# One kernel, one core: the last norm moved beside the last expert, and the down weights cut by FF tiles

## The chip, the cores and the metric

The kernel runs on one core of a Trainium2 chip. The metric is the device time of one execution in microseconds (us). TensorE (PE) multiplies, ScalarE (ACT) and VectorE (DVE) work on tiles, GpSimd (POOL) issues the indexed DMAs and now and then works on a tile, SyncE (SP) issues the other DMAs. Each engine runs its own instructions in program order and waits on semaphores.

## The reference

A two-layer backbone over 1024 latent and 256 context tokens of width D = 1024. What matters here is the second layer's mixture of experts and the last norm:

```python
aff = softmax(h @ router_w)                  # 1024 tokens, 16 experts
g, idx = top_k(swapaxes(aff, 1, 2), 128)     # each expert takes 128 tokens
xe = h[idx]
a, u = xe @ w_gate[e], xe @ w_up[e]          # 1024 -> 1408
y = (silu(a) * u) @ w_down[e]                # 1408 -> 1024
out = zeros.at[idx].add(y * g)
xl = xl + m_l[5] * out
return rmsnorm(xl, final_g)                  # per token: x / sqrt(mean(x*x) + eps) * final_g
```

A token can be taken by several experts or by none. Everything is float32; each product is made of three float32r products (high by high, high by low, low by high parts).

## The kernel before

The kernel is a row of stages with a barrier between them. The last three are choose_stage (top-k of the second layer, with FirstPieces beside it), expert_rows_stage (16 experts, called a turn each) and final_stage (the last norm).

In expert_rows_stage an expert's weights come as 12 pieces of 128x2816 words: a gate and an up piece for each of 4 units of 352 hidden columns, and four down pieces, each all 11 FF tiles by a quarter of the 1024 output columns. SP loads a piece into one of 5 raw places as soon as DVE has split the piece that lay there (L2235). ACT rounds it to its high part (L2360) and DVE subtracts to get the low part (L2421), into one of 4 places that PE frees four pieces later. PE takes the pieces in the order written in turn (L2332): gate 0, up 0, the four down pieces of the expert before, then gate and up of units 1 to 3. An up piece is 8 x 3 matmuls of 352 columns (L2288), a down piece 11 x 3 of 256 columns (L2304).

Between them stand transposes: turn_h (L2308) turns a unit's hidden rows h, and is followed by copy_h on ACT and split_h on DVE; it waits for multiply on DVE (L2433). turn_x (L2321) turns the gathered rows of the next expert, in the middle of the down pieces; copy_x and high_x on ACT and split_x on DVE (L2427) make its parts, double-buffered. POOL gathers the rows of expert e+1 (L2246) and scatters the weighted result of expert e-1 with an accumulating DMA into x_res in HBM (L2251); weigh on DVE (L2452) makes that result.

After the last scatter and a barrier, final_stage loads x_res in 8 tiles of 128 tokens into two places, squares and sums on ACT (L2854), takes the root on ACT (L2856), scales and multiplies on DVE (L2871, L2873) and stores.

Of the kernel before, what the change touches and what calls it, by code (L numbers as in the profile page):

```python
# [2092 lines left out]
ROW_UNITS, ROW_SLOTS, ROW_RAW = 4, 4, 5  # L2093
ROW_READY = ROW_SLOTS + ROW_RAW
ROW_U = FF // ROW_UNITS
ROW_PIECE = K * ROW_U
assert ROW_PIECE == FJ * (D // 4)


class RowBuffers:  # L2100
# [3 lines left out]
    def __init__(self, nc, ctx, m):  # L2104
# [3 lines left out]
        self.xg, self.xm = sb("xg", [P, D]), sb("xm", [P, D])  # L2108
        self.ys, self.gates = sb("ys", [P, D]), sb("gates", [P, D])
        self.x_hi, self.x_lo = (sb(x, [P, 2, K, P], F32R) for x in ("xhi", "xlo"))  # L2110
        self.h = sb("h", [P, FF])
        self.hT_hi, self.hT_lo = (sb(x, [P, FJ, P], F32R) for x in ("hthi", "htlo"))
        self.sa = m.rope[:, 0, 0:2 * ROW_U].rearrange("p (b n) -> p b n", b=2)
        self.gcur = sb("gcur", [P, 2])


class FirstPieces:
# [7 lines left out]

    def on_sync(self, sp):
        for n in range(ROW_READY):
# [4 lines left out]
            sp.dma_start(self.m.rows.raw[:, s, :], self.d["moe_rows"][n if n < 8 else 12]).then_inc(self.landed[s], 16)  # L2132
        for s in range(ROW_RAW):
            sp.wait_ge(self.landed[s], 16 * len(range(s, ROW_READY, ROW_RAW)))

    def on_scalar(self, act):
        r = self.m.rows
        for s in range(ROW_SLOTS):
            act.wait_ge(self.landed[s], 16)
            act.copy(r.high[:, s, :], r.raw[:, s, :]).then_inc(self.high_done, 1)  # L2140

    def on_gpsimd(self, pool):
        r = self.m.rows
        for s in range(ROW_SLOTS):
            pool.wait_ge(self.high_done, s + 1)
            pool.tensor_tensor(r.low[:, s, :], r.raw[:, s, :], r.high[:, s, :].bitcast(F32), ALU.subtract).then_inc(
                self.low_done, 1)
# [14 lines left out]
def expert_rows_stage(nc, m, d, name, layer):  # L2162
    UNITS, U, PIECE, SLOTS = ROW_UNITS, ROW_U, ROW_PIECE, ROW_SLOTS
    TURN = 12
    DOWN = range(2, 6)
    GROUPS = [range(0, 2), range(2, 5), range(5, 8), range(8, 11)]
    pieces = d["moe_rows"]
# [3 lines left out]
    with stage_of(nc) as ctx:  # L2171
        piece_done, high_done, low_done, sa_done, h_done, h_turned, hT_high, hT_low = semaphores(
            nc, ctx, " ".join(f"{name}_{x}" for x in "piece high low sa h hturn hthi htlo".split()))
        x_turned, x_read, x_high, x_low, y_read, ys_ready, gate_ready = semaphores(
            nc, ctx, " ".join(f"{name}_{x}" for x in "xturn xread xhi xlo yread ys gcur".split()))
        gates_in, gathered, scattered, x_parts = semaphores(
            nc, ctx, " ".join(f"{name}_{x}" for x in "gates gat scat xparts".split()))
# [3 lines left out]
        def prepared(e, p):  # L2181

            return isinstance(e, int) and e == 0 and p in (0, 1, 6, 7)

        def exists(e, p):

            return not isinstance(e, int) or (0 <= e < NE and not (e == 0 and p in DOWN)) or (e == NE and p in DOWN)

        def number(e, p):

            if isinstance(e, int) and e == 0 and p < DOWN[0]:
                return p + 1
            return e * TURN + (p + 1 - len(DOWN)) - (DOWN[0] if isinstance(e, int) and e == NE else 0)

        def before(e, p, places):

            while True:
                e, p = (e, p - places) if p >= places else (e - 1, p - places + TURN)
                if isinstance(e, int) and e < 0:
# [4 lines left out]
        def raw(e, p):  # L2204

            return r.raw[:, (number(e, p) - 1) % ROW_RAW, :]

        def landing(e, p):

            return piece_in[(number(e, p) - 1) % ROW_RAW], 16 * ((number(e, p) - 1) // ROW_RAW + 1)  # L2210

        def need(engine, sem, value):

            if value is not None and (not isinstance(value, int) or value > 0):
                engine.wait_ge(sem, value)

        def turns(engine, body):

            for e in range(NE + 1):
                body(e, e % 2)  # L2220

        def later(e):
# [788 lines left out]
```

## Time and profile before

| what | us |
|---|---|
| median of 3 runs | 3142.82 (3140.67 to 3143.96) |
| the profiled execution | 3143.25 |
| its span, first to last instruction | 3141.4 |
| PE busy in the span | 2829.9 (90%) |
| DVE, ACT, POOL busy | 2077.3, 1767.9, 630.1 |

The span is the stretch that the trace shows; the time of that execution is 1.85 us longer. A busy share is an average over stages with different limits, so each stage is read by itself.

### The profile page before, as it was taken

How to read it: one execution, taken by the hardware profiler on the slowest of the kernel's cores; microseconds unless marked ns; L12 is line 12 of the kernel's file. 1: busy time of each engine (PE TensorE's matmuls, PEld its weight loads, DVE VectorE, ACT ScalarE, POOL GpSimd, SP SyncE). 2: the span in 40 equal slices, each digit the busy share in tenths (PEclk: the TensorE clock that was granted, in tenths of full speed). 3: DMA queues.
4: the chain of work that ended last, by engine and by line, in shares of the span. 5: the costliest groups of instructions: out<-in, count | busy, mean ns of one | idle time of the engine just before them, and what ended most of it. 6: DMA issues, size and time to landing. Idle time of an engine off the chain costs nothing. (4 is left out here: it accounts for less than half of the span.)

```text
span 3141.4 us, 54667 instructions
## 1 busy us (share of the span) xinstructions
PE 2829.9 (90%) x23207; PEld 2423.5 (77%) x23207; DVE 2077.3 (66%) x2141; ACT 1767.9 (56%) x1876; POOL 630.1 (20%) x282
## 2 busy tenths in 40 slices
PE   6999897966999999999999689989469999999992
PEld 4788654755888888888888577757369999999992
DVE  3412555455677777777777358764668888888884
ACT  3111345443565656555655358874457777777764
POOL 3111232211111111111111056542301011011110
PEclk8999999987999999999999799999789999999996
DMA  5011362446887788778877410104569999999993
GB/s 218 28 40 32 145 229 77 148 165 234 302 309 285 284 310 309 286 282 309 311 286 276 169 34 31 41 13 166 195 229 366 388 377 369 391 369 381 380 364 121
DMA packets 139221, 726.41 MB, mean 231 GB/s; under 512 B 12226, under 2 KB 14946, under 8 KB 111202
## 3 DMA queue, kind: packets, MB, share of 16 engines
q1 hardware_dynamic: 126276, 684.99, 57.0%
q0 software_dynamic: 12288, 37.75, 4.8%
q8 instruction: 185, 3.03, 0.4%
q14 instruction: 56, 0.46, 0.0%
q10 hardware_dynamic: 416, 0.18, 0.0%
HBM read 680.90 MB, written 41.98 MB: 230 GB/s over the span
## 5 line engine op out<-in xcount | busy, mean ns | idle before, releaser
L1990 DVE TENSOR_TENSOR mixed_low<-mixed_raw,mixed_high 128x4096 fp32r<-128x4096 f32 (+1 forms) x142 | 576.4, 4059 | 216.9 <-ACT mixed_high L1920 216.8
L2421 DVE TENSOR_TENSOR rows_low<-rows_raw,rows_high 128x2816 fp32r<-128x2816 f32 x188 | 580.9, 3090 | 92.5 <-ACT rows_high L2360 88.6
L1920 ACT CAST mixed_high<-mixed_raw 128x4096 fp32r<-128x4096 f32 (+1 forms) x142 | 473.9, 3337 | 124.2 <-DMA mixed_raw<-in_moe 74.8
L2360 ACT CAST rows_high<-rows_raw 128x2816 fp32r<-128x2816 f32 x188 | 481.1, 2563 | 88.1 <-PE ps L2275 88.1
L2273 PE MATMUL ps<-rows_high,rows_xhi 128*128 128x352 f32 x1024 | 336.5, 329 | 4.5 <-issue 4.5
L2275 PE MATMUL ps<-rows_high,rows_xlo 128*128 128x352 f32 x1024 | 329.6, 322 | 0.0
L2274 PE MATMUL ps<-rows_low,rows_xhi 128*128 128x352 f32 x1024 | 328.8, 321 | 0.0
L1821 PE MATMUL ps<-mixed_high,mixed_xhi 128*128 128x512 f32 (+1 forms) x768 | 296.1, 386 | 3.5 <-DVE mixed_xlo L2006 3.5
L1822 PE MATMUL ps<-mixed_low,mixed_xhi 128*128 128x512 f32 (+1 forms) x768 | 286.6, 373 | 0.0
L1823 PE MATMUL ps<-mixed_high,mixed_xlo 128*128 128x512 f32 (+1 forms) x768 | 286.5, 373 | 0.0
L2273 PE MATMUL ps<-rows_high,rows_hthi 128*128 128x256 f32 x704 | 201.4, 286 | 3.0 <-issue 3.0
L2251 POOL DMA_INDIRECT x_res<-rows_ys,idx x16 | 68.0, 4249 | 677.8 <-DVEq L2455 677.8
L2274 PE MATMUL ps<-rows_low,rows_hthi 128*128 128x256 f32 x704 | 200.1, 284 | 0.0
L2275 PE MATMUL ps<-rows_high,rows_htlo 128*128 128x256 f32 x704 | 200.1, 284 | 0.0
L2273 PEld LDWEIGHTS ps<-rows_high,rows_xhi 128*128 128x128 f32 x1024 | 192.9, 188 | 4.9 <-issue 4.9
L2274 PEld LDWEIGHTS ps<-rows_low,rows_xhi 128*128 128x128 f32 x1024 | 193.6, 189 | 0.0
L2275 PEld LDWEIGHTS ps<-rows_high,rows_xlo 128*128 128x128 f32 x1024 | 192.5, 188 | 0.0
L1821 PEld LDWEIGHTS ps<-mixed_high,mixed_xhi 128*128 128x128 f32 x768 | 144.9, 189 | 41.8 <-issue 23.4
L1773 POOL DMA_INDIRECT x_res<-mixed_ys,idx x16 | 25.6, 1602 | 725.9 <-DVEq L2062 725.9
L1809 PE MATMUL ps<-mixed_raw,mixed_xc 128*32 128x128 f32 (+1 forms) x6144 | 164.0, 264 | 0.0
L1809 PEld LDWEIGHTS ps<-mixed_raw,mixed_xc 128*32 128x32 f32 x6144 | 152.0, 110 | 15.3 <-issue 15.3
L1823 PEld LDWEIGHTS ps<-mixed_high,mixed_xlo 128*128 128x128 f32 x768 | 144.8, 189 | 20.9
(351 smaller groups left out, 6282.5 us busy)
## 6 DMA issues: line engine op xcount, KB each, us to landing
rows_raw<-in_moe_rows SPq DMA_DIRECT2D x192, 1408.0 KB, 8.7
mixed_raw<-in_moe SPq DMA_DIRECT2D x96, 2048.0 KB, 12.5
mixed_raw<-in_moe SPq DMA_DIRECT2D x48, 1536.0 KB, 11.5
ring_r<-in_ada_w SPq DMA_DIRECT2D x19, 2048.0 KB, 8.0
mixed_raw<-in_ada_w SPq DMA_DIRECT2D x5, 2048.0 KB, 9.9
w_raw_r<-in_ev_in SPq DMA_DIRECT2D x18, 512.0 KB, 3.5
w_raw_u<-in_od_in SPq DMA_DIRECT2D x16, 512.0 KB, 3.7
x_res<-x_o SPq DMA_DIRECT2D x10, 512.0 KB, 2.6
```

Of the source, the lines that this page charges most:

```text
L1809: mm = pe.matmul(out, r.xc[:, owner % 2, k, :], w[:, :, k * P + 32 * g:k * P + 32 * g + 32], start=(k == 0), stop=(k == K - 1), tile_posit ...
L1821: pe.matmul(out, x_high_part, w_high_part, start=first, stop=False)
L1822: pe.matmul(out, x_high_part, w_low_part, start=False, stop=False)
L1823: return pe.matmul(out, x_low_part, w_high_part, start=False, stop=last)
L1920: act.copy(r.high[:, p % SLOTS, 0:nj, :], raw(e, p)).then_inc(high_done, 1)
L1990: dve.tensor_tensor(r.low[:, p % SLOTS, 0:nj, :], raw(e, p), r.high[:, p % SLOTS, 0:nj, :].bitcast(F32), ALU.subtract).then_inc(low_done, 1)
L2251: pool.indirect_dma_start(d["x_res"], bass.IndirectOffsetOnAxis(ap=m.idx[:, e:e + 1], axis=0), ys[:, :], None, compute_op=ALU.add).then_in ...
L2273: pe.matmul(out, x_high_part, w_high_part, start=first, stop=False)
L2274: pe.matmul(out, x_high_part, w_low_part, start=False, stop=False)
L2275: return pe.matmul(out, x_low_part, w_high_part, start=False, stop=last)
L2360: act.copy(high[:, p % SLOTS, :], raw(e, p)).then_inc(high_done, 1)
L2421: dve.tensor_tensor(low[:, p % SLOTS, :], raw(e, p), high[:, p % SLOTS, :].bitcast(F32), ALU.subtract).then_inc(low_done, 1)
```

## The change

The down weights of an expert are now cut by FF tiles into pieces of 2, 3, 3 and 3 tiles by all 1024 columns (the HBM layout stays, so a piece is loaded as 4 blocks of 2 or 3 KB per partition), and a matmul of a down piece is 512 columns wide. The order of pieces in a turn is gate 0, up 0, down 3 of the expert before, gate 1, up 1, down 0, gate 2, up 2, down 1, gate 3, up 3, down 2. turn_h follows each third piece; the two halves of turn_x follow the third and the sixth. The low part of x is single-buffered and made by POOL (low_x), but for expert 0, where DVE does it.

final_stage is gone. Beside the last expert, SP loads final_g and, after the scatter of the last expert but one, the 8 tiles of x_res into raw places that are free by then; ACT and DVE square them, DVE and POOL scale them, SP stores them. The last expert's result isn't scattered into x_res: POOL gathers its 128 rows of x_res, DVE adds and norms them (last_rows), and POOL writes them over the stored rows of out. FirstPieces loads 8 pieces (9 before) and splits 3 (4 before).

The diff, cut to its core:

```diff
+ROW_UNITS, ROW_SLOTS, ROW_RAW, ROW_SPLIT, ROW_TURN = 4, 4, 5, 3, 12
+ROW_READY = ROW_SPLIT + ROW_RAW
...
+ROW_J = [range(0, 2), range(2, 5), range(5, 8), range(8, 11)]
+ROW_PIECE = 3 * D
+QUARTER = D // 4
+ROW_GATE, ROW_UP, ROW_DOWN = (0, 3, 6, 9), (1, 4, 7, 10), (5, 8, 11, 2)
...
+def load_row_piece(sp, d, r, e, p):
+    kind, u = ROW_GROUP[p]
+    to = r.raw[:, (row_number(e, p) - 1) % ROW_RAW, 0:row_columns(p)]
+    if kind < 2:
+        return sp.dma_start(to, d["moe_rows"][e * 12 + 2 * u + kind])
+    at = (e - (p == 2)) * 12 + 8
+    j = ROW_J[u]
+    src = d["moe_rows"][at:at + 4, :, j[0] * QUARTER:(j[-1] + 1) * QUARTER].rearrange("q p n -> p q n")
+    return sp.dma_start(to.rearrange("p (q n) -> p q n", q=4), src)
...
+        self.x_hi, self.x_lo = sb("xhi", [P, 2, K, P], F32R), sb("xlo", [P, K, P], F32R)
+        self.hT_hi, self.hT_lo = (sb(x, [P, 2, 3, P], F32R) for x in ("hthi", "htlo"))
+        self.xm = m.rope[:, 1, :]
...
+        def last_place(i):
+            n = number(NE, 2) - 4 + i // 3
+            return n, r.raw[:, (n - 1) % ROW_RAW, (i % 3) * D:(i % 3 + 1) * D]
+        gain = last_place(0)[1]
+        tiles = [last_place(1 + t)[1] for t in range(LT)]
+        junk = xm
+        stat = m.mask[:, 0:4 * 16].rearrange("p (x t) -> p x t", x=4)
+        ON_DVE_SQUARE, ON_POOL = (2, 5), (1, 4, 7)
...
+            sp.wait_ge(low_done, splits(last_place(0)[0]))
+            sp.dma_start(gain, d["final_g"].to_broadcast((P, D))).then_inc(gain_in, 16)
+            sp.wait_ge(scattered, 16 * (NE - 1))
+            for t in range(LT):
+                sp.wait_ge(low_done, splits(last_place(1 + t)[0]))
+                sp.dma_start(tiles[t], d["x_res"][t * P:(t + 1) * P, :]).then_inc(x_in[t], 16)
+            for t in range(LT):
+                pooled = sum(x in ON_POOL for x in range(t + 1))
+                if t in ON_POOL:
+                    sp.wait_ge(out_pool, pooled)
+                else:
+                    sp.wait_ge(out_dve, t + 1 - pooled)
+                sp.dma_start(d["out"][t * P:(t + 1) * P, :], tiles[t]).then_inc(stored, 16)
+            sp.wait_ge(stored, 16 * LT)
...
+            def low_x(e):
+                pool.wait_ge(x_high, e + 1)
+                pool.wait_ge(piece_done, number(e - 1, ROW_UP[-1]))
+                flat = lambda x: x.rearrange("p k n -> p (k n)")
+                pool.tensor_tensor(flat(x_lo[:, :, :]), xm, flat(x_hi[:, e % 2, :, :]).bitcast(F32),
+                                   ALU.subtract).then_inc(x_low, 1)
...
+                if followed(e):
                     gather(e + 1)
                 if e:
                     scatter(e - 1)
-            scatter(NE - 1)
-            pool.wait_ge(scattered, 16 * NE)
+                if followed(e):
+                    low_x(e + 1)
+            pool.wait_ge(scattered, 16 * (NE - 1))
+            pool.wait_ge(x_turned, 2 * NE)
+            pool.indirect_dma_start(xg[:, :], None, d["x_res"], bass.IndirectOffsetOnAxis(
+                ap=m.idx[:, NE - 1:NE], axis=0)).then_inc(picked, 16)
+            pool.wait_ge(gain_in, 16)
+            pool.wait_ge(inverse_done, 1)
+            for t in ON_POOL:
+                pool.tensor_scalar(tiles[t], tiles[t], stat[:, 3, t:t + 1], None, ALU.mult).then_inc(chain, 1)
+                pool.wait_ge(chain, ON_POOL.index(t) + 1)
+                pool.tensor_tensor(tiles[t], tiles[t], gain, ALU.mult).then_inc(out_pool, 1)
+            pool.wait_ge(stored, 16 * LT)
+            pool.wait_ge(rows_added, 1)
+            pool.indirect_dma_start(d["out"], bass.IndirectOffsetOnAxis(ap=m.idx[:, NE - 1:NE], axis=0),
+                                    ys[:, :], None).then_inc(rows_out, 16)
+            pool.wait_ge(rows_out, 16)
             pool.wait_ge(gathered, 16 * NE)
...
+                    wh, wl = (w.rearrange("p (q j n) -> p j q n", q=4, n=QUARTER) for w in (wh, wl))
+                    steps = [(i, half) for i in range(len(ROW_J[u])) for half in range(2)]
+                    if e == NE:
+                        steps.sort(key=lambda step: step[1])
+                    for i, half in steps:
+                        j = ROW_J[u][i]
+                        at = slice(2 * half, 2 * half + 2)
+                        out = m.ps[:, 4 + half, :].rearrange("p (q n) -> p q n", q=2)
+                        mm = products(out, hT_hi[:, t % 2, i, :], hT_lo[:, t % 2, i, :],
+                                      wh[:, i, at, :], wl[:, i, at, :], j == 0, j == FJ - 1)
+                        if e == NE and (i, half) == (len(ROW_J[u]) - 1, 0):
+                            mm.then_inc(piece_done, 1)
...
+            for half in range(2):
+                turn_x(0, half)
+            for e in range(NE + 1):
+                for p in range(TURN):
+                    if exists(e, p):
+                        latent(e, p)
+                    if p % 3 == 2 and expert(e):
+                        turn_h(e, p // 3)
+                    if p in (2, 5) and followed(e):
+                        turn_x(e + 1, p // 3)
...
+                    t = UNITS * e + p // 3
+                    if p % 3 == 0 and 0 < t:
+                        copy_h(t - 1)
+                    if p % 3 == 0:
+                        silu(e, p // 3)
+                    if p in (4, 7) and followed(e):
+                        copy_x(e + 1, p // 7)
+                    if p == 8 and followed(e):
+                        high_x(e + 1)
+                    if followed(e) or p < 8:
+                        split(*following(e, p))
+                    if not followed(e) and p == 7:
+                        square(0)
+                        square(1)
+                    if not followed(e) and p == 8:
+                        split(NE, 2)
+                        square(3)
+            for t in (4, 6, 7):
+                square(t)
+            root(1, slice(0, LT))
+            copy_h(UNITS * NE - 1)
+            root(2, slice(LT, LT + 1))
...
+            def give(t):
+                dve.scalar_tensor_tensor(tiles[t], tiles[t], stat[:, 3, t:t + 1], gain, ALU.mult, ALU.mult).then_inc(out_dve, 1)
+            def last_rows():
+                part_sum = lambda i: stat[:, i, LT + 1:LT + 2]
+                dve.wait_ge(gate_ready, NE)
+                dve.wait_ge(picked, 16)
+                for half in range(2):
+                    at = slice(half * BANK, (half + 1) * BANK)
+                    dve.wait_ge(piece_done, number(NE, 2) + half)
+                    dve.scalar_tensor_tensor(ys[:, at], m.ps[:, 4 + half, :], gcur[:, 0:1], gates[:, at],
+                                             ALU.mult, ALU.mult).then_inc(y_read, 1)
+                    dve.wait_ge(y_read, e * 2 + half + 1)
+                    dve.tensor_tensor(xg[:, at], xg[:, at], ys[:, at], ALU.add).then_inc(y_read_b, 1)
+                    dve.wait_ge(y_read_b, 2 * half + 1)
+                    dve.tensor_tensor_reduce(ys[:, at], xg[:, at], xg[:, at], 1.0, 0.0, ALU.mult, ALU.add,
+                                             part_sum(half)).then_inc(sq_dve, 1)
+                    dve.wait_ge(sq_dve, len(ON_DVE_SQUARE) + half + 1)
+                    if half == 0:
+                        dve.tensor_scalar(part_sum(2), part_sum(0), 1.0 / D, EPS, ALU.mult, ALU.add).then_inc(y_read_b, 1)
+                        dve.wait_ge(y_read_b, 2)
+                dve.scalar_tensor_tensor(stat[:, 1, LT:LT + 1], part_sum(1), 1.0 / D, part_sum(2), ALU.mult, ALU.add).then_inc(
+                    mean_done, 1)
+                inverse(2, slice(LT, LT + 1))
+                dve.scalar_tensor_tensor(ys[:, :], xg[:, :], stat[:, 3, LT:LT + 1], gain, ALU.mult, ALU.mult).then_inc(
+                    rows_added, 1)
...
+            first_x()
+            dve.wait_ge(gates_in, 16)
+            for p in range(SLOTS):
+                split(0, p)
+            for e in range(NE):
                 for p in range(TURN):
+                    t = UNITS * e + p // 3
+                    if p % 3 == 0 and 0 < t:
+                        split_h(t - 1)
+                    if not followed(e) and p == 10:
+                        square(5)
+                    if p % 3 == 1:
+                        multiply(e, p // 3)
+                    if p == 2 and 0 < e:
+                        weigh(e - 1)
+                    if followed(e) or p < 8:
+                        split(*following(e, p))
+                    if not followed(e) and p == 8:
+                        dve.wait_ge(scattered, 16 * (NE - 1))
+                        square(2)
+                        split(NE, 2)
+            dve.wait_ge(y_read, 2 * (NE - 1))
+            dve.tensor_copy(gcur[:, 0:1], m.gate[:, NE - 1:NE]).then_inc(gate_ready, 1)
+            dve.wait_ge(sq_act, LT - len(ON_DVE_SQUARE))
+            dve.wait_ge(sq_dve, len(ON_DVE_SQUARE))
+            dve.tensor_scalar(stat[:, 1, 0:LT], stat[:, 0, 0:LT], 1.0 / D, EPS, ALU.mult, ALU.add).then_inc(mean_done, 1)
+            dve.wait_ge(gain_in, 16)
+            inverse(1, slice(0, LT))
+            give(0)
+            split_h(UNITS * NE - 1)
+            for t in range(1, LT):
+                if t not in ON_POOL:
+                    give(t)
+            last_rows()
...
-            (m.plain, lambda: final_stage(nc, m, d)),
```

## Rows read from the trace of the kernel before

**Rows 1.** The page: span, and busy time, share and instructions of PE.

```profile
span 3141.4 us, 54667 instructions
...
PE 2829.9 (90%) x23207; PEld 2423.5 (77%) x23207; DVE 2077.3 (66%) x2141; ACT 1767.9 (56%) x1876; POOL 630.1 (20%) x282
```

**Rows 2.** Busy time by stretch, one turn: PE, PEld, DVE, ACT, POOL, clock, DMA share, GB/s.

```profile
2390.83:2439.53 48.70, 48.70 (x346) 48.39 (x344) 42.80 (x25) 37.20 (x30) 6.94 (x2) 1.00 0.98 372
```

**Rows 3.** Timeline of POOL in the experts: start, us, what, idle before.

```profile
2464.08 4.42 POOL L2251 DMA_INDIRECT x_res<-rows_ys,idx  x1 [41.44 <-DVEq L2455]
2468.80 2.53 POOL L2246 DMA_INDIRECT rows_xg<-x_norm,idx  x1 [0.30 <-issue]
...
2999.76 4.43 POOL L2251 DMA_INDIRECT x_res<-rows_ys,idx  x1 [41.49 <-DVEq L2455]
```

**Rows 4.** Timeline of PE: 256 columns here, 512 in the first layer.

```profile
3030.33 0.28 PE L2273 MATMUL ps<-rows_high,rows_hthi 128*128 128x256 f32 x1
...
3040.05 0.28 PE L2273 MATMUL ps<-rows_high,rows_hthi 128*128 128x256 f32 x1
...
1252.59 0.39 PE L1821 MATMUL ps<-mixed_high,mixed_hthi 128*128 128x512 f32 x1
...
1255.54 0.39 PE L1822 MATMUL ps<-mixed_low,mixed_hthi 128*128 128x512 f32 x1
```

**Rows 5.** Groups of instructions, experts: busy us, mean ns, idle before, releasers.

```profile
L2421 DVE TENSOR_TENSOR rows_low<-rows_raw,rows_high 128x2816 fp32r<-128x2816 f32 x188 | 580.9, 3090 | 92.5 <-ACT rows_high L2360 88.6 <-DVE rows_ys L2452 3.2
L2360 ACT CAST rows_high<-rows_raw 128x2816 fp32r<-128x2816 f32 x188 | 481.1, 2563 | 88.1 <-PE ps L2275 88.1
L2433 DVE TENSOR_TENSOR rows_h<-ps,rope_sb 128x352 f32<-128x352 f32 x64 | 33.2, 518 | 11.3 <-PE ps L2275 9.5 <-issue 1.8
```

**Rows 6.** Timelines of DVE and POOL where the two meet.

```profile
2467.39 3.09 DVE L2421 TENSOR_TENSOR rows_low<-rows_raw,rows_high 128x2816 fp32r<-128x2816 f32 x1
...
2096.23 1.49 DVE L2763 SCALAR_TENSOR_TENSOR B_second<-B_second 128x1280 f32<-128x1280 f32 x1 [11.69 <-POOL B_second L2714]
2097.64 3.03 DVE L2784 TENSOR_TENSOR C_second<-C_second,B_second 128x1024 f32<-128x1024 f32 x1
...
2096.32 3.26 POOL L2709 TENSOR_TENSOR B_second<-B_second 128x1024 f32<-128x1024 f32 x1
```

**Rows 7.** Groups of POOL's instructions on tiles, other stages.

```profile
L537 POOL TENSOR_TENSOR w_lo_u<-w_raw_u,w_hi_u 128x1024 fp32r<-128x1024 f32 x12 | 28.8, 2399 | 20.4 <-ACT w_hi_u L532 20.4
...
L1093 POOL TENSOR_SCALAR A_r<-A_r,C_first 128x640 f32<-128x640 f32 x16 | 29.9, 1886 | 59.9 <-DVE C_first L1131 59.9
```

**Rows 8.** The gathers of either layer: duration min/median/max in ns; issue to landing.

```profile
L2246 POOL DMA_INDIRECT rows_xg<-x_norm,idx x16: 947/2510/2536, 2289.6 to 2955.8; - x16
...
DMA to landing us min/median/max: 4.3/15.9/17.2
...
L1766 POOL DMA_INDIRECT mixed_xg<-x_norm,idx x16: 947/1009/1723, 738.8 to 1615.7; - x16
...
DMA to landing us min/median/max: 4.2/5.8/7.5
```

**Rows 9.** DMA from 2400 to 2900 us: rate in 40 slices, one queue, weight loads.

```profile
GB/s 378 306 389 424 411 277 405 421 383 307 420 420 356 317 423 407 357 325 425 413 345 333 429 406 339 347 424 407 327 355 425 406 316 373 424 395 304 378 422 403
...
q1 hardware_dynamic: 17778, 178.02, 89.5%
...
rows_raw<-in_moe_rows SPq DMA_DIRECT2D x123, 1408.0 KB, 8.7
```

**Rows 10.** Timelines of PE, SP and DVE, the end; groups of the last norm.

```profile
3067.27 0.32 PE L2275 MATMUL ps<-rows_high,rows_xlo 128*128 128x352 f32 x1
...
3103.88 0.81 SPq L2829 DMA_DIRECT2D A_s<-x_res  x2
...
3136.65 1.23 DVE L2873 TENSOR_TENSOR A_s<-A_s 128x1024 f32<-128x1024 f32 x1
...
L2854 ACT ACTIVATE A_s<-A_s 128x1024 f32<-128x1024 f32 x8 | 8.4, 1055 | 7.3 <-DMA A_s<-x_res 7.3
```

More of the change, by code:

```diff
@@ L2162, in expert_rows_stage @@
 def expert_rows_stage(nc, m, d, name, layer):
[L2163 to L2167, printed above, removed]
+    UNITS, U, SLOTS, TURN = ROW_UNITS, ROW_U, ROW_SLOTS, ROW_TURN
+    exists, number = row_exists, row_number
     r = m.rows
@@ L2349, in _ @@
-            turn_x(0)
-            turns(pe, turn)
+                if kind == 0:
+                    need(pe, h_done, t - 1)
+                elif kind == 2:
+                    pe.wait_ge(hT_high, t + 1)
+                    pe.wait_ge(hT_low, t + 1)
+                    if u == 0:
+                        need(pe, y_read, e * 2)
+                need(pe, high_done, splits(number(e, p)))
+                need(pe, low_done, splits(number(e, p)))
+                wh, wl = (w[:, part(e, p), 0:row_columns(p)] for w in (high, low))
@@ L2354, in split @@
             def split(e, p):
-                if not exists(e, p) or prepared(e, p):
-                    return
-                act.wait_ge(*landing(e, p))
-                need(act, piece_done, before(e, p, SLOTS))
-                act.copy(high[:, p % SLOTS, :], raw(e, p)).then_inc(high_done, 1)
+                if exists(e, p) and number(e, p) > ROW_SPLIT:
+                    sem, value = landing(e, p)
+                    need(act, sem, value)
+                    need(act, piece_done, part_freed(e, p))
+                    act.copy(high[:, part(e, p), 0:row_columns(p)], raw(e, p)).then_inc(high_done, 1)
             def copy_x(e, half):
@@ new lines, in square, with root @@
+            def square(t):
+                act.wait_ge(x_in[t], 16)
+                done = sum(x not in ON_DVE_SQUARE for x in range(t))
+                if done:
+                    act.wait_ge(sq_act, done)
+                else:
+                    act.wait_ge(x_low, NE)
+                act.activation(junk, tiles[t], ACT.Square, accum_out=stat[:, 0, t:t + 1]).then_inc(sq_act, 1)
+            def root(n, at):
+                act.wait_ge(mean_done, n)
+                act.activation(stat[:, 2, at], stat[:, 1, at], ACT.Sqrt).then_inc(root_done, 1)
@@ L2429, in multiply @@
-            def multiply(e, p, u):
-                dve.wait_ge(sa_done, e * UNITS + (u + 1))
-                dve.wait_ge(piece_done, number(e, p))
-                need(dve, h_turned, (e - 1) * UNITS + (min(u + 1, 3) + 1))
+                if exists(e, p) and number(e, p) > ROW_SPLIT:
+                    dve.wait_ge(high_done, splits(number(e, p)))
+                    need(dve, piece_done, part_freed(e, p))
+                    dve.tensor_tensor(low[:, part(e, p), 0:row_columns(p)], raw(e, p),
+                                      high[:, part(e, p), 0:row_columns(p)].bitcast(F32), ALU.subtract).then_inc(low_done, 1)
```

390 lines of the change are left out of this document (144 added, 246 removed).

## The prediction

> **What bounds the kernel now.** I read four views: the page, then the busy times of one turn, then the waits of that turn, then its ends. The page gives PE 90% of the span [rows 1], which is a mean over stages and decides nothing. The scatters of the experts lie (2999.76 − 2464.08) / 11 = 48.70 us apart [rows 3], and in a window of that length PE is busy for all of it, at the full clock, while DVE has 42.80 and ACT 37.20 [rows 2]. So PE sets the turn, and DVE has about 6 us of slack. The groups agree: ACT's casts wait for PE to free a place and never for a DMA; DVE's splits wait for ACT, hardly for a landing [rows 5]. The DMA engines are busy 98% [rows 2], which looks like a bound, but a turn's 372 GB/s x 48.7 us = 18.1 MB would take 42.7 us at the 424 GB/s of the best slice [rows 9]: they are full because the queue runs ahead. The other thing to see is the end: the last up piece ends at 3067.27 + .16 = 3067.4 and the span at 3141.4, 74.0 us later, filled by four down pieces, a scatter, a barrier and the last norm, whose first load is issued only at 3103.88 [rows 10]. So a gain can come from PE's work in a turn and from these 74 us; the losses can come from whatever makes PE wait.
>
> **PE's work.** A matmul of 256 columns takes (3040.05 − 3030.33) / 81 = .120 us, one of 512 columns (2.95 / 13) = .227 [rows 4]. An expert's down pieces are now 4 x 33 = 132 of the first, 15.84 us, and become 11 x 2 x 3 = 66 of the second, 14.98: .86 less. Up to the last up piece PE did 15 experts' down pieces, 237.6 us; now it does these and 5 of 11 FF tiles of the last expert, 15.45 x 14.98 = 231.5. That is **−6.1**. Up pieces and the number of transposes stay.
>
> **Edit A, low_x on POOL.** The low part of x is now single-buffered, so it can be made only when up 3 of the expert before has ended, and gate 0 of the next expert waits for it. Between them lie one down piece of 3 tiles (18 x .227 = 4.1) and a turn_h, about 4.4 us. A POOL subtract of this shape and type took 2.40 [rows 7], which would fit. But POOL and DVE hold each other up when both read two tiles: a POOL multiply whose start a DVE step of 1.49 had preceded lasted 3.26, about 1.9 beyond that step's end, and the DVE multiply beside it lasted 3.03 instead of the 1.23 of the same size at the end [rows 6, 10]. DVE's splits are such steps, 3.09 long [rows 5], and run nearly back to back. In my hand schedule of the new turn up 3 ends at 43.5 us, the split then running goes from 42.6 to 45.7, low_x takes 45.7 to 48.0 and gate 0 could start at 47.6. I take .5 us for each of the 15 followed turns: **+7.5**. Lower bound: no wait, 0. Upper: low_x lasts 3.09 + 2.40 + its share of a second split, some 6.4 against 4.4, 2 us a turn, +30. I stay near the lower, because a POOL step that came second got in right behind the running one [rows 6]. The split behind low_x slips to 51.3, and DVE has the slack for it.
>
> **Edit B, the gather.** In the new POOL order a turn's scatter is followed by low_x, and then by the next gather, so the gather starts up to 3 us after gate 0. A gather takes .95 alone and 2.5 in the experts [rows 8], where its typical neighbour is a split: that of 2468.80 lasts until .9 behind the end of the split that began at 2467.39 [rows 3, 6]. I take it that the split holds it, so it ends near 4.1 us into the turn. The first half of turn_x needs the rows at 11.9, so 7.8 us are left. Now the gather lands 15.9 from its issue, 13.4 from its end, but it stands on its queue directly behind a scatter; in the first layer, without one, 5.8 [rows 8]. Alone under this load I estimate 4.8 to 8.4 (above: half way from 5.8 − 1.0 to the loaded value): **0**; the bound above is the rival below. The Trainium skill, page "SBUF — State Buffer", section "Who interferes with whom", agrees with edit A (a DVE instruction with two SBUF inputs contends with a GpSimd instruction that reads SBUF) but infers that a tensor_tensor doesn't hold up descriptor generation; the 2.5 against .95 speaks against that. By the page the gather would end some 2 us earlier; the sum would be the same.
>
> **Edit C, turn_h behind a short piece.** Each turn_h now follows one down piece after its up piece. Three of these last 4.1, but that of down 0 only 12 x .227 = 2.7. The multiply of .52 on DVE may stand behind a split of 3.09 that has just begun [rows 5], so the wait lies between 0 and .9. I take .25 a turn, 16 turns: **+4**. The rest of the order keeps PE fed: four split places are still freed one piece at a time, with pieces of 2.7 to 4.1 us against 3.09 of a split.
>
> **Edit D, loads in blocks.** A down piece comes as 4 blocks of 2 or 3 KB per partition instead of one of 11 KB. No row shows such blocks. The weights' queue takes 89.5% of the DMA engines' time [rows 9], 43.6 us a turn, a third of it for the down pieces. If smaller blocks cost 0 to 10% more, that is 0 to 1.5 us of DMA time in a turn of 48, and the 42.7 above leaves room: 0.
>
> **The start.** One piece fewer is split beforehand and x of expert 0 is made by DVE in halves; a split less behind choose_stage is cover lost, a half of x earlier is gained. I take **−.7**, bounds −2 to +2.
>
> **The tail.** From the end of the last up piece to the end it was 74.0. The scatter of expert 14 lands in the first half of the last turn, so the x_res tiles are loaded and squared beside up pieces 2 and 3. I count from the end of the last up piece. The inverse roots are there at about 5.3 (three squares of about 1.1, a root, DVE's reciprocal, behind the last split). Then POOL does three tiles, a TENSOR_SCALAR of 1.886 x 1024 / 640 = 3.0 at most (I take 2.85, since part is fixed) and a TENSOR_TENSOR of 2.0 (the 1.9 above) each [rows 6, 7], and DVE five of 1.25 [rows 10]; they alternate, so their sum counts: 14.6 + 6.2 = 20.8, plus .6 of semaphores, until 26.7. The last two down pieces end at 11.4, under this. last_rows adds about 5.2 on DVE (two halves of weigh, add, square at some .6 each, then 1.25): 31.9. The store of the last tile is then out, and the indexed write takes one issue and a landing like the shortest gather's, 4.2 to 4.9 [rows 8]: 36.8. So 74.0 becomes 37: **−37**. Bounds: 30, if POOL and DVE run beside each other (20.8 becomes 14.6); 50, if tiles come 8.7 late as a loaded weight piece does [rows 9] and the last matmuls run at half clock.
>
> **Sum.** −6.1 + 7.5 + 4 − .7 − 37 = −32.3. On the span 3141.4 [rows 1] that gives 3109.1, and with the 1.85 outside it 3111. The profiled execution is .4 above the median shown, so I say 3110.
>
> **Rivals.** *Late gather (the other side).* If the gather lands 13.4 after its end even without a scatter ahead of it, PE waits 13.4 − 7.8 = 5.6 us in 14 turns, 78 us: 3110 + 78 = 3188. For it: the DMA engines are 98% full, and a gather's packets stand in line with weights. Against: the scatter that stood ahead of it is gone. It decides from a wait of 33 / 14 = 2.4 us, a landing 10.2 after the end of the issue. *The lock costs nothing.* The waits of edit A are 0 and the tail is 30: 3110 − 7.5 − 7 = 3096. For it: low_x can fall between two splits; against: rows 6. *DMA becomes the bound.* Blocks of 2 to 3 KB cost more than estimated, 1 to 2 us a turn: 3125 to 3140. The groups' casts would then wait for raw tiles, which none does now [rows 5]. *The overlap at the end is partly lost*: the tail is 45 to 50, 3118 to 3123. *The change does not do what it says*: that would need loads of x_res that still start after the last piece, for a place or for a landed scatter; they wait for splits of the last pieces, which come early, and for the scatter of expert 14, so I give it nothing apart from the case before.
>
> **How the numbers follow.** Chances: forecast .55 (3110, its own range 3102 to 3118), lock free .17 (3096), late gather .12 (3130 to 3188), DMA bound .08, lost overlap .08. The range 3090 to 3130 holds the forecast, the lock-free case, the lost overlap and a part of the DMA case, about 8 in 10. A measurement of this kernel tells from no change about .2%, 6.3 us: faster is below 3136.5. Faster: forecast, lock free, lost overlap, most of the DMA case and a small part of the gathers, .84; same .05 (the rest of the DMA case and gathers that wait 2 to 3 us); slower .11 (gathers).
>
> **What would show it.** PE's down matmuls 512 wide at .227; distance of the scatters 47.9 to 48.6 (by the sum: 48.70 − .86 + .75 = 48.6); gate 0 waiting for POOL's low_x by about .5 us, and turn_h(1) for a multiply; no wait of PE for the transposed x at the third piece (a wait of 2 us or more there, ended by the gather's DMA, is the late gather); ACT's casts not waiting for raw tiles (waits there are the DMA case); POOL and DVE alternating over the scaled tiles, and 37 us from the last up matmul to the end. I am wrong if the tail is above 50 or if any wait comes back in every turn at above 2 us.

## The result and the profile after

The changed kernel takes 3106.68 us (median of 4 runs, 3105.96 to 3109.65) against 3141.74 (4 runs, 3140.37 to 3143.96): a ratio of 0.9884, 95% interval 0.987 to 0.9898, so 35 us less. The forecast was 3110, with 3102 to 3118 for its likeliest case.

The busy times by stretch show where. A row is the time from the end of choose_stage's last DVE instruction to gate 0 of expert 0, from there to the end of the last up piece, and from there to the end. Columns as in [rows 2]. Before:

```profile
2288.14:2301.16 13.02, 1.97 (x9) 1.60 (x9) 1.23 (x1) 5.23 (x10) 1.99 (x2) 0.50 0.39 121
2301.16:3067.43 766.27, 763.54 (x5345) 758.16 (x5345) 658.02 (x371) 573.61 (x447) 100.05 (x29) 1.00 0.95 365
3067.43:3141.40 73.97, 19.02 (x137) 18.44 (x135) 32.24 (x41) 28.87 (x36) 1.55 (x1) 0.65 0.39 128
```

After:

```profile
2284.52:2296.56 12.04, 1.97 (x9) 1.60 (x9) 2.60 (x6) 3.83 (x6) 1.98 (x2) 0.50 0.41 130
2296.56:3067.45 770.89, 765.29 (x4385) 712.72 (x4385) 677.12 (x361) 581.28 (x456) 145.20 (x45) 1.00 0.97 371
3067.45:3104.12 36.67, 10.79 (x41) 8.13 (x39) 24.33 (x26) 6.26 (x13) 19.88 (x7) 0.68 0.35 138
```

The three stretches change by −1.0, +4.6 and −37.3 us; together 853.3 becomes 819.6, −33.7. Of the 33.7, more than all lies behind the last up piece. The span changes by as much as that last stretch alone (3141.4 to 3104.1), because 3.6 us were already there when choose_stage ended, in code that is the same; for the same reason the last up piece ends at the same time as before (3067.4). That part differs from one execution to the next: in the profiled executions below choose_stage ends between 2284 and 2296. So parts of 2 to 6 us are read below from these stretches; the median of a kernel does not tell them apart.

One turn from gate 0 to gate 0, to be held against [rows 2]:

```profile
2879.51:2927.94 48.43, 48.32 (x277) 44.96 (x278) 43.21 (x24) 36.83 (x30) 9.82 (x3) 1.00 0.99 379
```

PE is still busy all but .11 of the turn in these columns, which count overlapped matmuls as busy; DVE has grown by .4 although it no longer makes the low part of x, POOL by 2.9. The small waits are read from starts. The first lines of PE are the end of the piece of two tiles with the turn_h behind it, the last those at the end of a turn, ahead of gate 0 (L2365 of form 128x352):

```profile
2902.20 0.39 PE L2367 MATMUL ps<-rows_high,rows_htlo 128*128 128x512 f32 x1
2902.58 0.55 PE L2412 MATMUL ps<-ident_sb,rows_h 128*128 128x128 f32 x3
...
2927.11 0.39 PE L2367 MATMUL ps<-rows_high,rows_htlo 128*128 128x512 f32 x1
2927.34 0.49 PE L2412 MATMUL ps<-ident_sb,rows_h 128*128 128x128 f32 x3
2927.94 0.40 PE L2365 MATMUL ps<-rows_high,rows_xhi 128*128 128x352 f32 x1
```

A turn_h that waits for nothing begins .23 behind the last matmul of 512 columns (2927.34 − 2927.11, one matmul's spacing). That at 2902.58 begins .38 behind: .15 lost, in all 16 turns 2.3 us. Gate 0 begins 2927.94 − 2927.34 = .60 after three transposes have begun; elsewhere a piece begins .03 behind the start of the last of such transposes, here .38, and in the 15 followed turns together 5.9 us are lost. The profile names no engine as the releaser here; what PE waits for is seen on the other two engines. At the turn_h it is DVE's multiply (L2551), which stands behind a split and ends at 2902.53, .05 ahead of the turn_h:

```profile
2899.00 3.09 DVE L2530 TENSOR_TENSOR rows_low<-rows_raw,rows_high 128x2816 fp32r<-128x2816 f32 x1 [1.36 <-ACT rows_high L2446]
2902.01 0.52 DVE L2551 TENSOR_TENSOR rows_h<-ps,rope_sb 128x352 f32<-128x352 f32 x1
```

At gate 0 it is POOL's low_x (L2333); POOL, with the gather and the scatter behind it:

```profile
2923.53 4.31 POOL L2333 TENSOR_TENSOR rows_xlo<-rope_sb,rows_xhi 128x1024 fp32r<-128x1024 f32 x1 [27.80 <-PE ps L2367]
2927.99 3.92 POOL L2319 DMA_INDIRECT rows_xg<-x_norm,idx  x1
2942.55 1.59 POOL L2324 DMA_INDIRECT x_res<-rows_ys,idx  x1 [10.63 <-DVEq L2573]
```

and DVE:

```profile
2922.49 3.09 DVE L2530 TENSOR_TENSOR rows_low<-rows_raw,rows_high 128x2816 fp32r<-128x2816 f32 x1 [0.94 <-ACT rows_high L2446]
2925.50 0.52 DVE L2551 TENSOR_TENSOR rows_h<-ps,rope_sb 128x352 f32<-128x352 f32 x1
2926.27 7.79 DVE L2530 TENSOR_TENSOR rows_low<-rows_raw,rows_high 128x3072 fp32r<-128x3072 f32 x2 [0.25 <-ACT rows_high L2446]
...
2942.60 3.09 DVE L2530 TENSOR_TENSOR rows_low<-rows_raw,rows_high 128x2816 fp32r<-128x2816 f32 x1 [0.39 <-ACT rows_high L2446]
```

low_x is asked for at 2923.53, inside a split that ends at 2922.49 + 3.09 = 2925.58, and ends at 2927.84, 2.26 behind it: about the 2.40 of [rows 7], behind a wait for the split. All 15 of them end 2.25 or 2.26 us behind the split in which they were asked for, and last 4.30 to 4.36. Gate 0 follows .10 later. The split that DVE starts at 2926.27 pays too: two splits last 7.79 instead of the 6.36 that such a pair takes in experiment 1. The multiply between them, whose one input lies in ps, takes its usual .52.

The late gather shows once. turn_x waits here, in one turn of 14; behind it stand the landings of all 16 gathers, counted from the start of the issue:

```profile
2601.26 0.66 PE L2423 MATMUL ps<-ident_sb,rows_xg 128*128 128x128 f32 x4 [0.56 <-DMA rows_xg<-x_norm,idx]
```

```profile
DMA to landing us min/median/max: 4.2/10.5/12.7
```

The end, first POOL, then DVE:

```profile
3073.72 3.87 POOL L2351 TENSOR_SCALAR rows_raw<-rows_raw,mask_sb 128x1024 f32<-128x1024 f32 x1 [22.11 <-DVE mask_sb L2583]
3077.66 2.40 POOL L2353 TENSOR_TENSOR rows_raw<-rows_raw 128x1024 f32<-128x1024 f32 x1
...
3090.47 2.34 POOL L2353 TENSOR_TENSOR rows_raw<-rows_raw 128x1024 f32<-128x1024 f32 x1
3096.87 1.04 POOL L2356 DMA_INDIRECT out<-rows_ys,idx  x1 [4.06 <-DVE rows_ys L2613]
```

```profile
3073.58 1.28 DVE L2587 SCALAR_TENSOR_TENSOR rows_raw<-rows_raw,mask_sb 128x1024 f32<-128x1024 f32 x1
3077.67 10.01 DVE L2587 SCALAR_TENSOR_TENSOR rows_raw<-rows_raw,mask_sb 128x1024 f32<-128x1024 f32 x4
3088.38 0.83 DVE L2602 TENSOR_TENSOR rows_xg<-rows_xg,rows_ys 128x512 f32<-128x512 f32 x1
3090.95 2.41 DVE L2602 TENSOR_TENSOR rows_xg<-rows_xg,rows_ys 128x512 f32<-128x512 f32 x1
3094.75 1.28 DVE L2613 SCALAR_TENSOR_TENSOR rows_ys<-rows_xg,mask_sb,rows_raw 128x1024 f32<-128x1024 f32 x1
```

The first scaling, begun ahead of POOL's, takes 1.28; the four beside POOL 10.01 / 4 = 2.5 in the mean, but one by one 3.47, 2.13, 1.27 and 3.35. The first and the last of them begin beside a TENSOR_TENSOR of POOL and end 1.1 behind its end; the two in the middle begin inside a TENSOR_SCALAR of POOL and do not wait for its end, one of them running at its usual speed. The second add of last_rows takes 2.41 and ends .55 behind POOL's last TENSOR_TENSOR (3092.81).

### The profile page after: what moved, and what is told of

Its sections match the earlier page's. It is cut to its first block and busy times, and to the rows that moved or that the text cites. A ratio compares the mean times of both kernels' runs of the same rounds, so it can differ in the third digit from the quotient of the medians.

```text
span 3104.1 us, 52492 instructions
## 1 busy us (share of the span) xinstructions
PE 2816.3 (91%) x22151; PEld 2364.4 (76%) x22151; DVE 2097.2 (68%) x2120; ACT 1748.5 (56%) x1855; POOL 690.3 (22%) x303
## 5 line engine op out<-in xcount | busy, mean ns | idle before, releaser
L2530 DVE TENSOR_TENSOR rows_low<-rows_raw,rows_high 128x2816 fp32r<-128x2816 f32 x189 | 603.2, 3205 | 91.2 <-ACT rows_high L2446 91.2
L2365 PE MATMUL ps<-rows_high,rows_xhi 128*128 128x352 f32 x1024 | 337.0, 329 | 6.2 <-DVE rows_xlo L2544 3.9
L2365 PEld LDWEIGHTS ps<-rows_high,rows_xhi 128*128 128x128 f32 x1024 | 193.5, 189 | 9.7 <-issue 9.7
L2333 POOL TENSOR_TENSOR rows_xlo<-rope_sb,rows_xhi 128x1024 fp32r<-128x1024 f32 x15 | 65.1, 4342 | 437.3 <-PE ps L2367 437.3
L548 PE MATMUL ps<-h_hi_r,w_hi_r 128*128 128x512 f32 (+1 forms) x432 | 157.8, 365 | 3.4 <-POOL h_lo_r L484 3.4
L1823 PEld LDWEIGHTS ps<-mixed_high,mixed_xlo 128*128 128x128 f32 x768 | 144.9, 189 | 20.8
L1822 PEld LDWEIGHTS ps<-mixed_low,mixed_xhi 128*128 128x128 f32 x768 | 145.3, 189 | 18.3
L549 PE MATMUL ps<-h_lo_r,w_hi_r 128*128 128x512 f32 (+1 forms) x432 | 153.8, 356 | 0.0
## 6 DMA issues: line engine op xcount, KB each, us to landing
mixed_raw<-in_moe SPq DMA_DIRECT2D x48, 1536.0 KB, 11.4
```

The source lines that it names most:

```text
L548: pe.matmul(out, wh, xh, start=(k == 0), stop=False)
L1822: pe.matmul(out, x_high_part, w_low_part, start=False, stop=False)
L1823: return pe.matmul(out, x_low_part, w_high_part, start=False, stop=last)
L2365: pe.matmul(out, x_high_part, w_high_part, start=first, stop=False)
L2530: dve.tensor_tensor(low[:, part(e, p), 0:row_columns(p)], raw(e, p), high[:, part(e, p), 0:row_columns(p)].bitcast(F32), ALU.subtract).the ...
```

## The experiments

All were measured beside the kernel before on chips where that one took 3144.8 (the first four kernels) and 3145.2 us (the others), so ratios are compared, and stretches of the profiled executions.

**1. The low part of x on DVE.** The lines taken out are POOL's, those put in DVE's.

```diff
-                if followed(e):
-                    low_x(e + 1)
...
                         multiply(e, p // 3)
+                    if p == 10 and followed(e):
+                        low_x(e + 1)
```

> DVE makes the low part of x for every expert, right behind the multiply of unit 3; POOL only gathers and scatters. The lock (my account): gate 0 waits in 15 turns, .42 us instead of .03, only because POOL's subtract stands .. behind DVE's split and lasts 4.3 us; on DVE it takes 1.23, so the waits go to .03, a turn goes from 48.43 to 48.05 and the time from 3106.7 to about 3101. The single buffer (rival): the low part can still only be made once up 3 has ended, so the wait stays and the time is 3106 to 3108. DVE late (rival): 1.2 us more on DVE in each turn delays the splits, PE waits for pieces, 3108 to 3115.

3106.97 us, ratio 0.988 (0.9865 to 0.9896): the median shows no difference. The stretch of the turns does, and DVE's line says why:

```profile
2308.56:3071.44 762.88, 760.07 (x4385) 710.63 (x4385) 671.54 (x376) 581.81 (x458) 73.56 (x30) 1.00 0.98 376
```

```profile
2834.88 0.52 DVE L2547 TENSOR_TENSOR rows_h<-ps,rope_sb 128x352 f32<-128x352 f32 x1
2835.31 1.22 DVE L2539 TENSOR_TENSOR rows_xlo<-rope_sb,rows_xhi 128x1024 fp32r<-128x1024 f32 x1
2836.44 6.36 DVE L2519 TENSOR_TENSOR rows_low<-rows_raw,rows_high 128x3072 fp32r<-128x3072 f32 x2
```

770.9 becomes 762.9, turns become 47.93, and the waits of gate 0 are gone (5.9 to 0). So it was not the single buffer; that on POOL it was the wait for the split, and not POOL's own 2.3 to 2.4 us, is shown by the ends 2.26 behind a split, for without that wait low_x would have ended about 1.7 us before gate 0 could begin. DVE's busy time falls, although it does more (677.1 to 671.5), for its splits are no longer held. turn_x waits in no turn: with no low_x ahead of it, the gather is issued as soon as the rows before are turned. Of the 8.0, 5.9 are these waits, .7 the late gather, and the rest, for the most part, the clock of unit 1's pieces in the first turn (experiment 4).

**2. POOL scales nothing at the end.**

```diff
-        ON_DVE_SQUARE, ON_POOL = (2, 5), (1, 4, 7)
+        ON_DVE_SQUARE, ON_POOL = (2, 5), ()
```

> DVE scales all eight tiles at the end, POOL none. The lock (my account): POOL's tiles are no help, for DVE's four scalings beside them last 2.5 instead of 1.28 and one add 2.41 instead of .83; DVE ends its eight near the time at which it ended its five, and the stretch behind the last up piece goes from 36.6 to about 34.2, the time from 3106.7 to about 3104. POOL helps (rival): three scalings more on DVE cost 3 x 1.28, 40 us behind the last up piece, 3110.

3107.42 us, 0.9884 (0.9869 to 0.99). The stretch behind the last up piece goes from 36.7 to 33.0, more than I expected:

```profile
2298.51:3072.86 774.35, 766.05 (x4385) 712.59 (x4385) 677.46 (x361) 581.64 (x457) 145.49 (x45) 1.00 0.97 370
3072.86:3105.81 32.95, 10.81 (x40) 8.13 (x39) 20.60 (x29) 5.94 (x12) 0.97 (x1) 0.71 0.39 156
```

```profile
3082.81 8.45 DVE L2587 SCALAR_TENSOR_TENSOR rows_raw<-rows_raw,mask_sb 128x1024 f32<-128x1024 f32 x7
3094.39 0.69 DVE L2602 TENSOR_TENSOR rows_xg<-rows_xg,rows_ys 128x512 f32<-128x512 f32 x1
```

Seven scalings take 8.45, less than the 10.01 of the four beside POOL: POOL's three tiles cost DVE more than they saved it. The stretch of the turns was 3.5 us longer in this execution, in the same instructions: turn_x waited for the gather in several turns (the starts behind the two transposes ahead of it add up to 5.5 us, 2.4 in the changed kernel, 1.6 where nothing waits).

**3. New pieces, old tail.** The stage of the last norm is put back and the last expert is scattered.

```diff
+            scatter(NE - 1)
+            pool.wait_ge(scattered, 16 * NE)
...
+            weigh(NE - 1)
...
+            (m.plain, lambda: final_stage(nc, m, d)),
```

> The new pieces, order and low_x with the last norm of before: the last expert is scattered into x_res and a stage of its own makes the norm. My account: the pieces alone cost, 4.6 us from the first gate piece to the last up piece, less 1.0 at the start; but only two instead of four down pieces are left behind the last up piece, so the stretch there goes from 74.0 to about 62; together about 3133. The pieces gain by themselves (rival, by the sum without waits): 3141.7 - 6.1 - 12 = 3124 or less. All comes from the norm beside the last expert (rival): 3141 to 3146.

3134.19 us (7 runs), 0.9968 (0.9956 to 0.9979).

```profile
2303.37:3073.55 770.18, 764.17 (x4386) 711.24 (x4387) 678.72 (x360) 578.88 (x451) 143.85 (x44) 1.00 0.96 365
3073.55:3132.97 59.42, 8.94 (x40) 6.88 (x39) 20.73 (x37) 21.45 (x33) 1.56 (x1) 0.63 0.47 159
```

The turns cost the same 770, so the loss of about 4 us there belongs to the new pieces, their order and low_x on POOL, not to the loads of x_res. Of the 37.3 at the end, 74.0 − 59.4 = 14.6 come from the order, which leaves two down pieces behind the last up piece instead of four (PE's busy time there falls from 19.0 to 8.9; the other 4.5 are waits of PE ahead of turn_h and the down pieces, which in the kernel before stood behind DVE's last splits), and 59.4 − 36.7 = 22.7 from the norm beside the last expert.

**4. First turn: multiply ahead of the split.**

```diff
-                    if p % 3 == 1:
+                    early = lambda e, p: e == 0 and p == 0
+                    if early(e, p):
+                        multiply(e, p // 3)
+                    if p % 3 == 1 and not early(e, p - 1):
                         multiply(e, p // 3)
```

> In the first turn alone, DVE takes the multiply of unit 0 ahead of the split of the fourth piece. My account: PE's stall of 3.1 us ahead of the first turn_h comes from the split that stands before the multiply and falls to about .9; if the low clock behind it (9.2 us for the two pieces instead of 7.6) comes from the stall too, that goes as well: 3106.7 becomes 3103; if the clock is low there anyway, 3104.5. The split is late next (rival): gate 1 or up 1 waits for what the multiply displaced, 3106 to 3108.

3106.42 us, 0.9883 (0.9867 to 0.9899). PE at the first turn_h, in the changed kernel and here:

```profile
2305.42 0.32 PE L2367 MATMUL ps<-rows_high,rows_xlo 128*128 128x352 f32 x1
2308.52 0.44 PE L2412 MATMUL ps<-ident_sb,rows_h 128*128 128x128 f32 x2 [2.77 <-DVE rows_h L2551]
```

```profile
2305.25 0.32 PE L2367 MATMUL ps<-rows_high,rows_xlo 128*128 128x352 f32 x1
2306.30 0.44 PE L2412 MATMUL ps<-ident_sb,rows_h 128*128 128x128 f32 x2 [0.72 <-DVE rows_h L2551]
```

The stall falls from 3.10 to 1.05 as said, and nothing is late next but .6 at the turn_h of unit 1 in the same turn. From first gate to last up piece it takes 767.6 instead of 770.9:

```profile
2296.07:3063.62 767.55, 764.03 (x4385) 711.02 (x4385) 677.19 (x361) 582.83 (x457) 145.55 (x45) 1.00 0.97 373
```

What follows the stall does not go as said: the gate and up pieces of unit 1 took 9.20 in the changed kernel and 7.55 here; but also 7.55 in experiment 3, whose first turn has the same instructions as the changed kernel's and the same stall (3.13). The two stretches behind that stall, the changed kernel's and then experiment 3's:

```profile
2309.15:2318.50 9.35, 9.35 (x51) 9.35 (x50) 5.57 (x4) 4.89 (x7) 0.00 (x0) 0.82 0.95 369
```

```profile
2315.90:2323.60 7.70, 7.70 (x52) 7.70 (x51) 5.51 (x4) 4.82 (x6) 0.00 (x0) 1.00 0.96 371
```

The granted clock is .82 in the one, a mean over its two levels of 1.2 and 2.4 GHz, and 1.00, the upper level throughout, in the other. So it differs between executions of the same code, and experiment 4 does not show that the stall sets it. Behind a stall of 3.1 the clock fell in three of the profiled executions (the changed kernel, experiments 2 and 6: 9.15 to 9.20) and stayed up in four (1, 3, 5 and 7: 7.55 to 7.66); behind one of 1.05 it stayed up in both (4 and 8). What decides it stays open.

**5. Unit 1: multiply ahead of the split.**

```diff
-                    if p % 3 == 1:
+                    early = lambda e, p: p == 3
+                    if early(e, p):
+                        multiply(e, p // 3)
+                    if p % 3 == 1 and not early(e, p - 1):
                         multiply(e, p // 3)
```

> In each turn DVE takes the multiply of unit 1 ahead of the split of piece 7 that stood before it. The split ahead (my account): turn_h after the piece of two tiles waits .15 us beyond the .23 of the others, 16 times, for a multiply behind a split; the 2.3 us go, 3106.7 becomes 3104.4 and the stretch from first gate to last up piece 770.9 becomes 768.6. The displaced split is late next (rival): up 2 or down 1 waits for it, no gain or a loss. The wait is that of the transposes for something else (rival, h_turned or hT_low): .38 stays.

3107.81 us, 0.988 (0.9863 to 0.9897). The .15 beyond the .23 is gone in all turns (the sum falls from 2.3 to under .1), as in this one:

```profile
2906.33 0.39 PE L2367 MATMUL ps<-rows_high,rows_htlo 128*128 128x512 f32 x1
2906.57 0.49 PE L2412 MATMUL ps<-ident_sb,rows_h 128*128 128x128 f32 x3
```

```profile
2304.35:3070.57 766.22, 760.20 (x4385) 711.86 (x4385) 673.77 (x360) 580.40 (x454) 145.50 (x45) 1.00 0.97 373
```

Turns without a late gather take 48.13 to 48.18, not 48.34 to 48.43. The stretch falls from 770.9 to 766.2, below the 768.6 expected, but part of that is not the edit's: unit 1 of the first turn took 7.66 here, not 9.20. Gate 0's waits rise a little, from 5.9 to 6.2. No split is late.

**6. Longer blocks.**

```diff
-    j = ROW_J[u]
-    src = d["moe_rows"][at:at + 4, :, j[0] * QUARTER:(j[-1] + 1) * QUARTER].rearrange("q p n -> p q n")
-    return sp.dma_start(to.rearrange("p (q n) -> p q n", q=4), src)
+    src = d["moe_rows"][at:at + 2, :, 0:len(ROW_J[u]) * BANK].rearrange("q p n -> p q n")
+    return sp.dma_start(to.rearrange("p (q n) -> p q n", q=2), src)
```

> Each down piece is loaded as two blocks of 4 or 6 KB per partition instead of four of 2 or 3 KB (other words of the same array, so the result of the down products is another). The blocks cost nothing (my account): no cast waits for a load, so turns stay at 48.3 to 48.4, 3106 to 3108. The loads set the turns a little (rival): turns fall by .3 us or more, under 3102. The shorter queue could bring the gathers in earlier: then only the .7 us of the one late gather goes.

3108.79 us, 0.989 (0.987 to 0.9911), and the turns stay:

```profile
2300.30:3071.21 770.91, 765.60 (x4385) 712.59 (x4385) 677.31 (x361) 581.81 (x457) 144.77 (x45) 1.00 0.96 372
```

**7. Gather ahead of low_x.**

```diff
             gather(0)
+            gather(1)
             for e in range(NE):
-                if followed(e):
-                    gather(e + 1)
                 if e:
                     scatter(e - 1)
+                if e + 2 < NE:
+                    gather(e + 2)
                 if followed(e):
                     low_x(e + 1)
```

> POOL issues the gather of the next but one expert before low_x, right when the rows before it have been turned, instead of behind it. The late gather (my account): the .7 us by which turn_x waited in one turn of the changed kernel, up to 4 us in other runs, go; the waits of gate 0 stay at .39 in 15 turns, so 3106 and, from first gate to last up piece, 770.2. The gather is what holds low_x up (rival): gate 0's waits fall as well, by up to 5.9 us, 3101.

3105.91 us, 0.9883 (0.9863 to 0.9904).

```profile
2295.95:3065.08 769.13, 764.21 (x4385) 711.53 (x4385) 677.21 (x361) 581.72 (x457) 138.40 (x45) 1.00 0.98 372
```

No turn_x waits (1.63, the floor), and low_x still takes 4.3 us, with 5.8 us of waits at gate 0. So the two losses are separate: one is POOL's order, the other POOL's arithmetic under DVE's splits.

**8. Together:** experiments 1, 2, 4 and 5, and three of DVE's scalings ahead of the last split_h. The lines are those of the last point alone.

```diff
-            give(0)
+            for t in range(3):
+                give(t)
             split_h(UNITS * NE - 1)
```

> low_x on DVE, the multiplies of unit 1 and of the first turn's unit 0 ahead of their splits, all eight last tiles scaled by DVE, three of them ahead of the last split_h. By my account the parts add: 5.9 (gate 0) + .7 (late gather) + 2.3 (unit 1) + 2.1 to 3.7 (first turn) + 3.7 (tail) + 1.5 (order of the scalings) = 16 to 18 from the end of choose_stage on, 819.6 becomes 802 to 804, the time about 3090 and the ratio to the kernel before about .983. If DVE becomes the bound of the turn (rival; it has 43.2 of 48.4 us, and 44.5 of 47.8 then), the turns stay at 48.0 or above and the sum falls short by 3 us or more.

3091.28 us (5 runs, 3090.1 to 3095.43), ratio 0.9835 (0.982 to 0.985).

```profile
2287.12:2299.09 11.97, 1.97 (x9) 1.60 (x9) 2.59 (x5) 3.83 (x6) 1.98 (x2) 0.50 0.41 130
2299.09:3056.28 757.19, 756.40 (x4385) 711.17 (x4385) 667.52 (x376) 580.41 (x454) 80.25 (x30) 1.00 0.99 378
3056.28:3088.31 32.03, 10.77 (x41) 8.12 (x39) 21.68 (x29) 7.05 (x14) 0.97 (x1) 0.72 0.42 166
```

801.2 from the end of choose_stage, against 802 to 804 expected and 819.6 in the changed kernel; a turn takes 47.73, and PE is busy for 756.4 of 757.2. The small parts, none of which its own median showed, add up to an effect that does.

## Why the prediction was right

| term | forecast, us | measured, us |
|---|---|---|
| start | −.7 | −1.0 |
| PE's down work, short of the last up piece | −6.1 | −5.7 |
| edit A, gate 0 waits for low_x | +7.5 | +5.9 |
| edit B, the gather | 0 | +.7 |
| edit C, turn_h behind the short piece | +4 | +2.3 |
| unit 1 of the first turn, partly at 1.2 GHz | none | +1.65 |
| first gate to last up piece | +5.4 | +4.6 |
| behind the last up piece | −37 | −37.3 |
| from the end of choose_stage | −32.3 | −33.7 |

The forecast, the likeliest of its cases, came true, and its rivals (a free lock, a late gather in every turn, DMA as the bound, an overlap lost at the end) did not, but for .7 us of the late gather. The median lies 3.3 us below 3110. Of these, 1.4 are the terms and 1.1 the kernel before, whose median was 3142.82 when the forecast was made and 3141.74 beside the changed kernel.

**PE's work** is right. By the starts within the pieces, the 1980 matmuls of 256 columns up to the last up piece are .1204 us apart in the kernel before, and the 1020 of 512 columns .2282 in the changed one: 238.5 and 232.8, next to the forecast's 237.6 and 231.5. With this −5.7 the terms of the turns add up to 4.9, measured as 4.6. PE's stall in the first turn is no term, for both kernels have it (2.73 before, 2.77 after). The spacing of 512 columns is the one that the first layer's rows gave [rows 4].

**Edit A** is right in place, mechanism and size: .39 a turn where .5 was taken; experiment 1 removed it, and experiment 7 shows that it isn't the gather. The bound of "no cost" would have held if low_x had begun between two splits, but all 15 were asked for inside one.

**Edit B** is right with little to spare. The issue ends 2883.49 − 2879.51 = 4.0 into the turn (forecast 4.1), turn_x comes 8.1 later (7.8), and the gathers land 6.1 to 8.8 behind the end of the issue (4.8 to 8.4; half way from 4.8 to the 13.4 of before would have been 9.1, so that upper bound was worked out wrong). So the rival of the late gather began to happen at its smallest: .7 in this execution, some 4 us in that of experiment 2, far from its 78. The 13.4 of before fits the scatter ahead on the queue: in the trace of before, packets of the scatter issued at 2464.08 and of the gather behind it run in one train from 2472.1 to 2484.9, and here those of a gather by themselves (2935.4 to 2938.2). No run puts the gather back right behind a scatter. What stands less well is what the prediction made of the Trainium skill, page "SBUF — State Buffer", section "Who interferes with whom". The gather at 2927.99, begun inside a split, ends .86 behind that split's end (2931.05), as the gathers of before did; the scatters of before, begun inside splits too, lasted 4.4 and ended 1.45 behind. But the scatter at 2942.55, begun .05 ahead of a split, takes 1.59, and that split its 3.09: neither holds the other. So it is in all 15 scatters (1.57 to 1.61). So in these traces a running split does not hold up an indexed DMA that has begun; it keeps one from starting. The Trainium skill's inference there, that tensor_tensor leaves descriptor generation alone, fits the scatter, and its rule on GpSimd instructions that read SBUF would cover the start if the row numbers, which lie in SBUF, are read then; no run here tells that apart.

**Edit C** cost a little over half of the price taken, .15 a turn for .25, within its bounds; experiment 5 shows the cause to be the split ahead of the multiply. **Edit D** costs nothing that half as many blocks of twice the length would win back (experiment 6), and no cast of ACT waits for a load.

**The tail** came out at its sum by luck in part: two steps were off by some 3 us each, in opposite directions. The roots were there at 6.1 (3073.54; forecast 5.3) and POOL was done at 25.4 (26.7). But last_rows did not wait for POOL: DVE's scalings ended at 20.2, before POOL's, and it ran beside POOL's last steps and ended at 3096.03, 28.6 instead of 31.9. (The last two down pieces ended at 14.8 instead of 11.4, still under the scalings.) From there the end took 8.1 instead of 4.9: the write is issued .8 later, lands 3.4 behind the start of its issue (3100.3), and then POOL drains for 2.7 us (3100.44 to 3103.18) before the stage can close. The term that failed in size is that write, priced by a gather's landing alone. In the kernel before the last store was SP's, whose drain took no time in the trace; but a drain of POOL's stands in that trace too, behind the last scatter, which lands at 3099.65: POOL drains from 3099.83 to 3102.49, and the forecast did not count it. That POOL and DVE hold each other up is shown by experiment 2, and the bound of 30 "if they run beside each other" is out. They do not alternate in full, though: the two scalings that began inside POOL's TENSOR_SCALAR ran beside it. And POOL's steps were priced too low, a TENSOR_SCALAR 3.8 to 3.9 long for 2.85 and a TENSOR_TENSOR 2.3 to 2.7 for 2.0, waits for DVE included; that the sum of 20.8 was nearly right (19.3 were measured from the roots to POOL's end) is luck too.

## What to carry to other kernels

Work given to an idle POOL was not free where DVE was reading two SBUF tiles at that time: three tiles on POOL made DVE's part longer than if it had done all, and a subtract of 1.2 us on DVE became 4.3 on POOL. An edit with several small costs and one large gain is best read by stretches between instructions that are in both traces, since the stages ahead differ by more than the small costs from run to run. And a second look at a gain's parts pays: 15 us more were to be had by taking low_x and the last scalings off POOL and moving two multiplies ahead of a split, against waits that the forecast had listed or the trace then showed.

## What the runs showed of the hardware

An indexed DMA on POOL that begins inside a DVE split with two SBUF inputs waits for its end (a gather 3.92 us long, ending .86 behind it), one that begins .05 us ahead of it does not (a scatter, 1.59), nor does it slow the split (3.09). POOL's subtract, asked for inside such a split, ended 2.25 to 2.26 behind the split all 15 times. A DVE multiply with one input in PSUM ran at its .52 inside POOL's subtract. An indexed DMA that ended a stage cost, beside its landing, a drain on POOL: 2.7 us behind the last write, 2.66 behind the last scatter of the kernel before. And the granted clock of the pieces behind a stall of 3.1 us was .82 in one execution and 1.00 in another of the same instructions.
